# Smaller matrix products in the last inverse level of a delta rule, and another form of one head norm

## What is computed

```python
tri = lower + jnp.eye(C, dtype=f32)
sol = lax.linalg.triangular_solve(tri, rhs, left_side=True, lower=True, unit_diagonal=True)
...
o = chunked_gated_delta_rule(q, k, v, g, beta).transpose(0, 2, 1, 3)
zh = z.reshape(B, L, DN_HEADS, DN_HEAD_DIM).astype(jnp.float32)
o = rms_norm(o, norm_w) * jax.nn.silu(zh)
return o.reshape(B, L, DN_WIDTH).astype(z.dtype) @ w_o
```

## Time and profile before

| what | us |
|---|---|
| median of three executions | 2530.85 |
| the profiled execution | 2530.36 |
| its span in the trace | 2528.5 |
| TensorE busy | 2470.7 |
| GpSimd busy | 1466.4 |
| ScalarE busy | 1249.4 |
| VectorE busy | 1153.8 |

### The profile page before, as it was taken

How to read it: one execution, slowest core, us unless ns; L and a number is a source line. 1 busy time by engine, 2 the same in 40 slices (tenths; PEclk the granted TensorE clock), 3 DMA queues, 4 the chain that set the end, 5 groups by cost and what they waited for, 6 DMA issues and landing times.

```text
span 2528.5 us, 42005 instructions
## 1 busy us (share of the span) xinstructions
PE 2470.7 (98%) x16572; PEld 2162.3 (86%) x16572; DVE 1153.8 (46%) x2116; ACT 1249.4 (49%) x2133; POOL 1466.4 (58%) x853
## 2 busy tenths in 40 slices
PE   7999999999999999999999999999999999999998
PEld 7998889998999889998677877778888878898998
DVE  8897544443978554536426522321101023535144
ACT  6458554455447764436554522453333345546543
POOL 6876746457976755556532344656565546564970
PEclk9999999999999999999999999999999999999999
DMA  6544344345544443345421112222222223245554
GB/s 244 182 167 167 129 156 151 134 184 184 186 167 165 151 167 129 139 154 201 150 83 51 51 67 104 84 101 99 100 84 100 98 102 134 84 142 192 184 184 150
DMA packets 50599, 347.62 MB, mean 137 GB/s; under 512 B 5360, under 2 KB 8688, under 8 KB 8944
## 3 DMA queue, kind: packets, MB, share of 16 engines
q1 hardware_dynamic: 47840, 340.31, 37.5%
q10 hardware_dynamic: 2576, 4.72, 0.6%
HBM read 343.96 MB, written 1.05 MB: 136 GB/s over the span
## 4 chain that ended last, share of the span: by engine, by line
PE 88%; ACT 4%; DVE 3%; POOL 2%; DMA 1%; issue 1%; ACTq 0%; DVEq 0%; SPq 0%; POOLq 0%
PE pg L1951 23%; PE pg L1953 22%; PE pg L1952 22%; PE ps L2272 2%; PE ps L2293 2%; PE ps L2291 1%; PE ps L2428 1%; PE pg L1974 1%; ACT ring_hi L798 1%; PE ps L2409 1%; PE ps L2122 1%; POOL ring_lo L669 1%; DMA ring<-in_w_stream_dram 1%; PE ps L2128 1%; PE ps L2097 1%
## 5 line engine op out<-in xcount | busy, mean ns | idle before, releaser
L669 POOL TENSOR_TENSOR ring_lo<-ring,ring_hi 128x1024 fp32r<-128x1024 f32 (+3 forms) x502 | 1173.4, 2354 | 693.1 <-ACT ring_hi L798 692.3
L1951 PE MATMUL pg<-HH,ring_hi 128*128 128x256 f32 (+1 forms) x3264 | 1036.7, 318 | 10.5 <-POOL ring_lo L669 4.4
L1952 PE MATMUL pg<-HH,ring_lo 128*128 128x256 f32 (+1 forms) x3264 | 990.3, 303 | 0.0
L1953 PE MATMUL pg<-HL,ring_hi 128*128 128x256 f32 (+1 forms) x3008 | 918.6, 305 | 0.0
L1951 PEld LDWEIGHTS pg<-HH,ring_hi 128*128 128x128 f32 x3264 | 617.3, 189 | 73.8 <-issue 35.0
L1952 PEld LDWEIGHTS pg<-HH,ring_lo 128*128 128x128 f32 x3264 | 617.5, 189 | 42.4 <-issue 15.5
L1953 PEld LDWEIGHTS pg<-HL,ring_hi 128*128 128x128 f32 x3008 | 568.6, 189 | 28.1
L798 ACT ACTIVATE ring_hi<-ring 128x1024 fp32r<-128x1024 f32 (+3 forms) x572 | 563.7, 1002 | 40.5 <-DMA ring<-in_w_stream_dram 39.4
L808 ACT ACTIVATE take<-pg 128x256 f32<-128x256 f32 (+1 forms) x242 | 104.0, 430 | 427.1 <-PE pg L1953 421.3
L1953 PE MATMUL pg<-big_r,ring_hi 128*128 128x256 f32 (+1 forms) x928 | 299.3, 322 | 0.0
L1951 PE MATMUL pg<-big_r,ring_hi 128*128 128x256 f32 (+1 forms) x752 | 246.1, 327 | 3.9 <-DVE ring_lo L1637 2.7
(11 more groups left out here) (346 smaller groups left out, 3313.6 us busy)
## 6 DMA issues: line engine op xcount, KB each, us to landing
ring<-in_w_stream_dram SPq DMA_DIRECT2D x320, 1024.0 KB, 4.8
hn<-in_consts_dram ACTq DMA_DIRECT2D x2, 1024.0 KB, 6.1
cst<-in_consts_dram SPq DMA_DIRECT2D x1, 1472.0 KB, 19.6
prm<-in_params_dram SPq DMA_DIRECT2D x1, 1110.0 KB, 9.5
X<-in_xT_dram SPq DMA_DIRECT2D x1, 1024.0 KB, 5.8
X<-in_ctxT_dram ACTq DMA_DIRECT2D x1, 1024.0 KB, 5.8
out_dram<-H ACTq DMA_DIRECT2D x4, 256.0 KB, 2.2
cst<-in_consts_dram SPq DMA_DIRECT2D x1, 768.0 KB, 16.5
```

The source lines that it names most:

```text
L669: pool.tensor_tensor(ring_lo[:, slot, cols], ring[:, slot, cols], ring_hi[:, place * P:(place + n) * P].bitcast(F32), SUB).then_inc(sem(LO ...
L1951: first = pe.matmul(out, a[0], b[0], start=start, stop=False)
L1952: pe.matmul(out, a[1], b[0], start=False, stop=False)
L1953: return first, pe.matmul(out, a[0], b[1], start=False, stop=stop)
```

## The change

In level 6 the products use rows 0 to 63 and columns 64 to 127 of each block only; the copy of X and the update of TT shrink to the same quarter (64 partitions, four times 64 columns). For the norm of the delta output, `pair_sums` multiplies each pair of heads (512 columns) with 32 columns of ones into its own 32 partitions of one bank. ScalarE takes Ln and Exp over that bank alone (128x512) into `rstd`. After the second gate chunk, `pair_roots` waits for that (`do_root`) and spreads each pair's row over 128 partitions, one product with a single row of ones for each bank.

```diff
@@ ScalarE, delta
-                    act.activation(XS, ps[:, 1, :], ACT.Copy).then_inc(sem("d_xs"), 1)
+                    if s < 6:
+                        act.activation(XS, ps[:, 1, :], ACT.Copy).then_inc(sem("d_xs"), 1)
+                    else:
+                        rows = lambda ap: ap.rearrange("p (a b) -> p a b", b=P)[HALF:P, :, 0:HALF]
+                        act.activation(rows(XS), rows(ps[:, 1, :]), ACT.Copy).then_inc(sem("d_xs"), 1)
@@ ScalarE, after the units
-                hn_root(HN_BASE1(l) + DO_N, 2048, 1.0 / P)
+                log_exp_tables()
+                act.wait_ge(sem("hn_ss"), HN_BASE1(l) + DO_N + 1)
+                act.wait_ge(sem("hn_done"), HN_BASE1(l) + DO_N)
+                inverse_root(rstd[:, :], ps[:, 0, :], eps6, 1.0 / P, "do_root")
@@ VectorE, delta
-                    dve.tensor_tensor(TT, TT, ps[:, 2, :], SUB).then_inc(sem("d_upd"), 1)
+                        dve.tensor_tensor(TT, TT, ps[:, 2, :], SUB).then_inc(sem("d_upd"), 1)
+                    else:
+                        cols = lambda ap: q4(ap)[0:HALF, :, HALF:P]
+                        dve.tensor_tensor(cols(TT), cols(TT), cols(ps[:, 2, :]), SUB).then_inc(sem("d_upd"), 1)
@@ TensorE
+            def pair_sums(l, squares):
+
+                pe.wait_ge(sem("hn_sq"), HN_BASE1(l) + DO_N + 1)
+                for g in range(4):
+                    ins = pe.matmul(ps[g * 32:(g + 1) * 32, 0, :], ones[:, 0:32], squares[:, 2 * g:2 * g + 2, :], start=True, stop=True)
+                ins.then_inc(sem("hn_ss"), 1)
+
+            def pair_roots(l):
+
+                pe.wait_ge(sem("do_root"), l + 1)
+                for g in range(4):
+                    ins = pe.matmul(ps[:, g, :], ones[g * 32:g * 32 + 1, :], rstd[g * 32:g * 32 + 1, :], start=True, stop=True)
+                ins.then_inc(sem("hn_rms"), 1)
...
-                        ins = pe.matmul(ps[:, 1, s], LM[v % 2][:, s], TM[:, s], start=True, stop=True)
+                        if v < 6:
+                            ins = pe.matmul(ps[:, 1, s], LM[v % 2][:, s], TM[:, s], start=True, stop=True)
+                        else:
+                            early, late = halves(s)
+                            ins = pe.matmul(ps[HALF:P, 1, early], LM[v % 2][0:HALF, late], TM[0:HALF, early], start=True, stop=True)
...
-                        ins = pe.matmul(ps[:, 2, s], XS[:, s], TT[:, s], start=True, stop=True)
+                        if v < 6:
+                            ins = pe.matmul(ps[:, 2, s], XS[:, s], TT[:, s], start=True, stop=True)
+                        else:
+                            early, late = halves(s)
+                            ins = pe.matmul(ps[0:HALF, 2, late], XS[HALF:P, early], TT[HALF:P, late], start=True, stop=True)
@@ TensorE, after the units
-                head_norm(HN_BASE1(l) + DO_N, 2048)
+                pair_sums(l, sq.rearrange("p (a b) -> p a b", b=T))
                 for x in gates[1:] + [("d_out", l, i) for i in range(1, 2 * KD, 2)]:
                     fill([x])
+                    if x == gates[1]:
+                        pair_roots(l)
```

More of the change, by code:

```diff
@@ L12 @@
 NT = T // P
+HALF = P // 2
 DEPTH = 2
@@ L2221, in delta_pair, with halves @@
                 return [(2 * u + p // 2, p % 2, slice(p * P, (p + 1) * P)) for p in range(4)]
+            def halves(s):
+                return slice(s.start, s.start + HALF), slice(s.start + HALF, s.stop)
             kT = lambda h, c: DN[:, HEADS + h, c * P:(c + 1) * P]
```

## The result

The changed kernel takes 2535.44 us (median of 20 runs; the kernel before on the same chip 2530.89, 20 runs). The ratio is 1.0016, 95% interval 1.0010 to 1.0023: slower by some 4 us. The forecast was 2534.0, its range 2527.5 to 2539.

The account below looks back on a forecast made before the run. The prediction took TensorE's own sequence and waits as the bound. From 2530.36 us, -2.1 (level 6), +3.7 (later modulation row) and +1.8 (clock) gave 2533.8, stated as 2534.0 against the median; range 2527.5 to 2539.

Parts of the forecast that it names:

- The bound: Whole kernel: TensorE's own sequence and its waits set the time; shorter ScalarE and VectorE copies give nothing by themselves.
- Level 6: Delta units: 16 groups of products at 0.76 us instead of 0.89, tile changes included, -2.1 us in all.
- Both groups of level 6 lie between full products: Delta units: each of the 16 groups therefore pays two tile changes, 0.33 us, leaving a gain of 0.13 each.
- Sums: Norm of the delta output: `pair_sums` takes 1.2 us on TensorE instead of 3.51, -2.3 us per layer.
- The wait: Behind the second gate chunk: TensorE stands for ScalarE's root, 3.2 us in layer 0 and 2.9 in layer 1.
- Roots: `pair_roots`: eight passes on separate row groups take 1.2 us; the modulation row then starts later, +3.7 us over both layers.
- one after another: Rival for `pair_roots`: its passes run serially, 3.5 us, adding 2.3 us per layer, total 2538.6; chance 0.12.
- The clock: TensorE behind each new wait: the granted clock falls, +0.9 us per layer, +1.8 in all; bounds -1.7 and +3.4 per layer.
- the second rival: Behind the waits: two clock falls in a row per layer, little hidden, 2.4 us more per layer, total 2538.8; chance 0.12.
- the forecast's shift of the row: Layer 0, modulation row behind the roots: it starts at 544.4 us instead of 542.38, +2.0 us.
- The sum: Whole kernel: 2530.36 - 2.1 + 3.7 + 1.8 = 2533.8 us, given as 2534.0.
- The fourth rival: Norm: root in time, TensorE waits under 0.5 us, norm costs 2.4 for 3.5 us; total 2526.1; chance 0.10.

Follow-up runs that it names:

- level 6 alone: The kernel before with only the edits of level 6, its norm the old one: 2528.22 us against 2531.12, ratio 0.9990.
- the norm alone: The kernel before with only the norm's edits, its level 6 the old one: 2536.56 us against 2531.12, ratio 1.0023.
- the roots behind the row: The changed kernel with `pair_roots` moved from behind the second gate chunk to behind the modulation row: 2527.36 us against 2531.35 before, ratio 0.9986.
- The reordered kernel: The changed kernel with ScalarE taking the root before it splits the next ring slot and drains the first gate chunk: 2523.74 us against 2531.12 before.
- a wait alone: The kernel before, old norm kept, with only a TensorE wait for the root added behind the second gate chunk: 2538.91 us against 2531.62, ratio 1.0027.
- the split group: Only level 6's edits, with each unit's X products cut in two halves, each followed by its transposes: 2531.96 us against 2531.35 before, ratio 1.0002.

## Why the prediction was right, step by step

**The bound** held: TensorE's sequence and its waits explain every kernel of the study, and the copies alone are worth nothing that the runs could tell.

**Level 6**: -2.1 was forecast, -2.9 measured. The traces give the same: in the kernel before, the delta units last from 345.7 to 533.0 and from 945.3 to 1132.4 us (first X product to last output product), 187.3 and 187.1; with level 6 alone 347.2 to 533.0 and 944.8 to 1130.5, 185.8 and 185.7: 2.9 us. The step mis-sized is "Both groups of level 6 lie between full products". That holds for ten of the 16. The X group in the last unit took 521.08 - 519.47 = 1.61 us in the kernel before, from the last L1951 ahead of it to the first behind its transposes; it gained 1.61 - 1.47 = 0.14 us, just as forecast. But in unit 0 of each layer the second group stands between two pieces of the modulation row, which is a small tile itself. Unit 0 of layer 0, TensorE's timeline, before and with level 6 alone:

```profile
379.98 1.05 PE L1974 MATMUL pg<-ring,prm 128*32 128x512 f32 x4
380.97 1.16 PE L2293 MATMUL ps<-big 128*128 128x128 f32 x8
381.96 0.60 PE L2296 MATMUL ps<-cst,big 128*128 128x128 f32 x4
382.49 1.91 PE L1974 MATMUL pg<-ring,prm 128*32 128x512 f32 x12
```

```profile
381.26 1.05 PE L1982 MATMUL pg<-ring,prm 128*32 128x512 f32 x4
382.25 0.67 PE L2327 MATMUL ps<-big 64*64 64x64 f32 x8
382.85 0.66 PE L2330 MATMUL ps<-cst,big 128*128 128x128 f32 x4
383.44 1.91 PE L1982 MATMUL pg<-ring,prm 128*32 128x512 f32 x12
```

The distance from one piece to the next falls from 2.51 to 2.18: 0.33, not 0.13. Four more groups, the first of unit 0 and the second of the last unit in each layer, stand between products with two moving columns (L2016) and such a piece; from the first of those products to the piece it is 2.31 us before and 2.08 with level 6 alone. Together that is 10 x 0.14 + 2 x 0.33 + 4 x 0.23 = 3.0 us. That the old kernel had already paid for a change of tile at these six places is the likely reason; no run tries it.

**Sums**: 1.2 forecast, 1.19 measured.

**The wait**: 3.2 and 2.9 us forecast, 3.23 and 3.5 measured (layer 0 and 1), at the place and for the reason given. Ln started 6.0 us behind the end of the first gate chunk, as before. Ln took 0.69 (0.66), Exp 0.63 (0.58). The 0.55 us too little in layer 1 are the ring's load. The step took its landing from the kernel before, where the split starts 1137.97 - 1132.42 = 5.55 us behind the delta units; in the changed kernel it is 1138.74 - 1132.69 = 6.05. Its chain has the load at

```profile
1133.23 5.48 DMA ring<-in_w_stream_dram
```

0.7 us longer than in layer 0. In the kernel with the norm alone that load took 6.57 us, and the wait was 4.5. ScalarE starts another load beside it (`W4`, in layer 1 alone), but the kernel before has that too; why the landing varies stays open.

**Roots**: 1.2 forecast with the changes of tile, 1.27 measured at full clock; the group's printed length is 1.14 there and 2.09 at half. The rival "one after another" (3.5) falls. The Trainium skill (the page "TensorE: Matmul & The Clock Gate", "Measured speedup vs the span model") gives 3.07 times for four row groups of 32 rows, from which the prediction had 1.1; the trace agrees for groups of one row: 3.4 / 1.14 = 3.0, taking the printed length.

**The clock**: this is the term that was too small. +0.9 per layer was taken, with +3.4 as a bound; two stretches in a row came behind each wait, as the second rival had it. In layer 0 the roots took 0.95 us more and the row 1.7 more. What is won back was foreseen in part: the prediction's clock section has the ring's 1.1 us partly absorbed, but its sum for the wait says that nothing is won back downstream. The waits for late low parts went from 4.6 to 2.5, and to 2.4 with the roots behind the row, where the clock did not fall. By the timelines, from the end of the delta units to the second tile of the gate chunk behind the row it is 544.69 - 533.0 = 11.7 before and 548.43 - 531.7 = 16.7 after, +5.0, of which 2.0 are the forecast's shift of the row at full clock, and 3.0 the clock. 1.1 of that the ring absorbs, so the clock cost about 1.9 net in this layer, twice what was taken. This is the reading of one execution. By windows of 1 us over its whole span, TensorE ran for 32.5 us at 0.50, and in the kernel before for 19.0. Behind the two waits lie 13.6 of these, in place of the 3.4 that layer 1 had before; a further stretch of 3.4 stands at 2327 us, far from the change, and whether it belongs to it isn't known.

**The sum**: by the runs, -2.9 for level 6 and +5.4 to +5.8 for the norm (+5.5 forecast, 3.7 + 1.8) against +4.5 measured for both. That the total came within 1.4 us is in part luck: level 6's gain (0.8 us too small) and the clock's loss (some 2 us too small by layer 0) erred in opposite directions. The fourth rival, "the change does what it says", named what was missing: ScalarE at its Ln before 540. The reordered kernel is just that, with the changed kernel's clock falls gone, and ran at 2523.7 where the rival was priced at 2526.1: 7.4 us under its before in place of 4.3, of which level 6 has 0.8. The rest lies inside the interval (3.8 to 9.1) and has no cause shown.

## What to carry to other kernels

When a result that only a slack engine needed is routed through the bounding engine, the wait moves onto that engine: look up when the result is there, on the other engine's timeline and in its order of issue, not how long its instructions take. Here the norm with the shorter root lost 5 us, and the same norm with the root issued ahead of a copy that had to wait for a load anyway won 3. A quarter-size product gained little where it was a lone small tile among full ones (0.14 us a group), and more next to other small tiles (0.23 to 0.33).

## What the runs showed of the hardware

- A wait of 3.2 to 3.5 us on TensorE was followed by up to 6.9 us at a mean granted clock of 0.52, with 1.92 us of products then taking 3.64; in the kernel with a wait alone by 3.4 us. Waits of 1.2 and 1.4 us, with the roots behind the row, were followed by no fall.
- Entering and leaving a 64\*64 tile between full products costs 0.28 us (the split group) to 0.33 us (rows 5) each time, even where transposes follow at once.
- Four products with one row of weights each, on four groups of rows and into four banks, run together: eight passes of 512 columns in 1.14 us.
- Halving the moving columns of float32 products to 64 with 128 weight columns gains next to nothing (0.83 us for 0.89 a group, ratio 1.0007); with 64 weight columns as well a pass takes 0.058 us in place of 0.111.
